# Two token halves pipelined in an eight-core decoder trunk: mixer or attention of one half interleaved with out-projection and FFN of the other

## The reference, cut to what matters

```python
# layer 1: Mamba-2 mixer, then ConvFFN; layer 2: attention, then ConvFFN
x = x + mamba2_mixer(rms_norm(x, a_norm), ...)   # in-proj to z,x,B,C,dt; causal conv of width 4; SiLU;
                                                 # chunked scan carrying a state over the tokens, 8 groups;
                                                 # gate with SiLU(z), group norm, out-proj 2048 -> 1024
x = x + conv_ffn(x, ...)                         # gate, val = rms_norm(x) @ w_in (1024 -> 2*2816)
                                                 # SiLU(causal conv of width 3 (gate)) * val, @ w_down
kv = rms_norm(x, kv_norm) @ w_kv + b_kv          # shared K/V, K normed and rotated
x = x + attention(...)                           # window 128, learned sinks, 16 query heads; out-proj
x = x + conv_ffn(x, ...)
```

## Time and profile before

| | |
|---|---|
| median of 3 runs | 2165.28 us (2155.01 to 2270.05) |
| profiled execution | 2161.5 us, span of its slowest core 2160.0 us |
| PE busy | 1840.8 us (85%) |
| DVE busy | 1266.3 us (59%) |
| ACT busy | 922.3 us (43%) |
| POOL busy | 578.7 us (27%) |
| chain that ended last | PE 66%, DMA 10%, DVE 8%, issue 7%, ACT 4% |

### The profile page before, as it was taken

One profiled execution on the slowest core, in us unless ns is written; L12 is line 12 of the kernel. 1 busy time (PEld: TensorE's weight loads), 2 busy tenths in 40 slices (PEclk: granted clock), 3 DMA queues, 4 the chain that ended last, 5 costly groups with the idle time before them and its releaser, 6 DMA issues.

```text
span 2160.0 us, 29050 instructions; the slowest of 8 cores (2109.5 to 2160.0 us)
## 1 busy us (share of the span) xinstructions
PE 1840.8 (85%) x9656; PEld 882.1 (41%) x9656; DVE 1266.3 (59%) x1863; ACT 922.3 (43%) x1380; POOL 578.7 (27%) x783
## 2 busy tenths in 40 slices
PE   1777887878878898999999995768587699999999
PEld 0344544545545443444444442223132344444444
DVE  2797787888878534653475324666567465325532
ACT  2557676757768313331133104564457333103310
POOL 2134464545645611000220022333222100000000
PEclk9898999999999999999999998989899899999999
DMA  9532343242335999543654449394853954375444
GB/s 206 129 60 52 52 71 53 44 68 51 52 61 137 194 163 126 98 79 64 110 91 78 74 78 102 59 108 68 69 88 64 93 88 78 64 156 83 78 74 112
DMA packets 220081, 193.05 MB, mean 89 GB/s; under 512 B 181408, under 2 KB 182688, under 8 KB 219936
## 3 DMA queue, kind: packets, MB, share of 16 engines
q0 software_dynamic: 32400, 115.42, 34.0%
q1 hardware_dynamic: 187536, 75.78, 21.2%
HBM read 254.65 MB, written 9.96 MB: 123 GB/s over the span
## 4 chain that ended last, share of the span: by engine, by line
PE 66%; DMA 10%; DVE 8%; issue 7%; ACT 4%; SPq 3%; POOL 2%; DVEq 0%; ACTq 0%; POOLq 0%
PE ps L238 66%; DMA hkv<-xnB_208 4%; SPq L324 3%; DMA hF_187<-xnF_191 2%; DVE acc_123 L278 2%; DMA hF_187<-xnF_190 1%; DVE acc_124 L278 1%; DVE att L267 1%; DMA xk_135<-xc_115 1%; SPq L317 0%; DMA yT<-yn_166 0%; DMA hT<-xnA_106 0%; DVE qT L267 0%; DVE dtot_211 L267 0%; DMA xin_84<-x 0%
## 5 line engine op out<-in xcount | busy, mean ns | idle before, releaser
L278 DVE SCALAR_TENSOR_TENSOR facc_192<-ps,cst,facc_192 128x1023 f32<-128x1023 f32 x88 | 112.8, 1281 | 60.7 <-ACT facc_192 L263 60.0
L278 DVE SCALAR_TENSOR_TENSOR facc_193<-ps,cst,facc_193 128x1023 f32<-128x1023 f32 x88 | 112.8, 1281 | 57.2 <-ACT facc_193 L263 56.4
L278 DVE SCALAR_TENSOR_TENSOR acc_123<-ps,cst,acc_123 128x1023 f32<-128x1023 f32 (+2 forms) x96 | 122.5, 1276 | 7.4 <-ACT acc_123 L263 7.3
L278 DVE SCALAR_TENSOR_TENSOR acc_124<-ps,cst,acc_124 128x1023 f32<-128x1023 f32 (+2 forms) x96 | 122.5, 1276 | 3.0 <-ACT acc_124 L263 2.3
L263 ACT ACTIVATE facc_192<-ps,cst 128x1024 f32<-128x1024 f32 x44 | 52.9, 1202 | 151.1 <-PE ps L238 151.1
L238 PE MATMUL ps<-cm 128*128 128x512 bf16 x252 | 102.2, 406 | 0.0
L263 ACT ACTIVATE sg_195<-facc_193 128x1024 bf16<-128x1024 f32 x44 | 46.5, 1057 | 129.9 <-DVE facc_193 L278 129.9
L263 ACT ACT_TABLE_LOAD x74 | 94.9, 1283 | 16.0 <-DVE acc_123 L278 8.8
L263 ACT ACTIVATE sg_194<-facc_192 128x1024 bf16<-128x1024 f32 x44 | 46.5, 1057 | 117.4 <-DVE facc_192 L278 117.2
L238 PE MATMUL ps<-hT,wr_60 128*128 128x512 bf16 x192 | 50.2, 406 | 52.4 <-DMA hT<-xnA_102 46.1
L267 DVE TENSOR_TENSOR u<-sg_195,ps 128x1024 bf16<-128x1024 bf16 x44 | 53.7, 1221 | 57.5 <-PE ps L238 50.3
(11 more groups left out here) (618 smaller groups left out, 4477.5 us busy)
## 6 DMA issues: line engine op xcount, KB each, us to landing
wr_63<-wfin POOLq DMA_DIRECT2D x18, 512.0 KB, 5.1
wr_61<-wfin POOLq DMA_DIRECT2D x18, 512.0 KB, 5.2
wr_62<-wfin POOLq DMA_DIRECT2D x18, 512.0 KB, 5.2
wr_64<-wfin POOLq DMA_DIRECT2D x17, 512.0 KB, 5.1
wr_60<-wfin POOLq DMA_DIRECT2D x17, 512.0 KB, 5.2
wr_60<-wfdn POOLq DMA_DIRECT2D x8, 512.0 KB, 5.1
wr_61<-wfdn POOLq DMA_DIRECT2D x8, 512.0 KB, 5.1
wr_62<-wfdn POOLq DMA_DIRECT2D x8, 512.0 KB, 5.1
```

The lines of the kernel that those rows point to most:

```text
L278: return self.add("dve", lambda e: e.scalar_tensor_tensor(out, in0, scalar, in1, op0, op1), rd, [out], self._c_dve(out, [in0, in1], "stt", ...
```

## The change

What it does, part by part:

1. Order. The mixer's units run half by half over all groups (`units` is now h outer, g inner). After the mixer of half 0 the program has four more stages: mixer half 1 with out-projection and FFN of half 0; attention blocks 0, 1 with out-projection and FFN of half 1; attention blocks 2, 3 with FFN of layer 2 of half 0; FFN of layer 2 of half 1 alone. All stage functions are generators that yield the modelled PE time of what they recorded; `inter` always advances the one that is behind.
2. PSUM. In a shared stage the FFN side has banks 0 to 3 (one pair for gate, one for value), the mixer or attention banks 4 to 7: one pair for P, bank 6 for decay, states and B-C products, bank 7 for y; attention has two banks for everything but the output.
3. Weights. Two rings, "A" with three slots and "F" with four. The mixer's 24 tiles are loaded once for each half.
4. `norm` scales with a tensor_scalar, transposes with 32 matmul transposes, and multiplies by the gain when PSUM is evacuated (ACT or DVE). Half 1 of the first norm keeps the DMA transpose (`norm_x`).
5. The FFN goes in thirds (8, 7, 7 channel tiles): gate, then a partial down-projection added to x; x is updated three times instead of once. The last FFN half keeps one pass and two pairs each.
6. Buffers: `xcB`, `bcB` two instead of three, head-norm sets two instead of four, one buffer for the rotary tables; scan states and y of half 1 go through HBM (`scr_st`, `scr_y`); K is stored by pairs of heads without zero padding.
7. The first x tiles are loaded ahead of the constants; the scheduler's modelled DMA costs are changed.

```diff
@@ schedule
-                if op.dma is not None:
+                if op.dmat:
+                    s0 = max(t + 0.45, dma_free)
+                    dma_free = s0 + op.dmat
+                    free_at[e] = max(t + c, s0 + 0.8)
+                    op.fin = dma_free + 1.3
+                elif op.dma is not None:
...
@@ weights
-    def wload(name, c0, n, shape):
-        slot = wcount[0] % NSLOT
+    def wload(name, c0, n, shape, ring="F"):
+        sl = rings[ring]
+        slot = wcount[ring] % len(sl)
...
+    def inter(*gens):
+        st = [[g, float(tot), 0.0] for g, tot in gens]
+        while st:
+            s = min(st, key=lambda v: v[2] / v[1])
+            w = next(s[0], None)
+            if w is None:
+                st.remove(s)
+                continue
+            s[2] += w
+            yield w
@@ norm
-                    K.stt(xv[:], tiles[i], rs[:, r, i:i + 1], grow, OP.mult, OP.mult)
-                    K.dmat(dst(i), xv[:], f"{sem}{i}")
+            K.ts(xn[i][:], tiles[i], rv[i], None, OP.mult)
+        for k2 in range(4):
+            pb = ps[:, nextbank(), :].bitcast(BF16).rearrange("p (k n) -> p k n", k=2)
+            for k in range(2):
+                for i in range(4):
+                    K.tr(pb[:, k, i * 128:(i + 1) * 128], xn[i][:, (2 * k2 + k) * 128:(2 * k2 + k + 1) * 128], ident)
+            for k in range(2):
+                for gname, dst in gains:
+                    K.evac(dst(2 * k2 + k), pb[:, k, :], scale=C(gname, 2 * k2 + k))
@@ mixer
-    units = [(g, h) for g in range(8) for h in range(2)]
+    units = [(g, h) for h in range(2) for g in range(8)]
+    PB = [(0, 1), (2,)]
+    SEG = [4, 6]
+    CBK = [7, 6]
+    wide = [True, False]
...
+    def A_gen(i0, i1):
+        for i in range(i0, i1):
+            if i == 6:
+                held["F"].extend([K.all_ops[-1]] * 4)
+            gens = [(S_gen(i), 10.4)]
+            if i + 1 < len(units):
+                gens.insert(0, (P_gen(i + 1), 20.8))
+            yield from inter(*gens)
@@ FFN
+    def gate(l, h, j, hb, uout, tg, tv):
+        w = wload(f"wfin{l}", j * 2048, 2048, (8, 256))
...
+    THIRDS = [(0, 8), (8, 15), (15, 22)]
+    def ffn_gen(l, h):
+        yield from norm_gen(l, h, hF)
+        for a, e in THIRDS:
+            for j in range(a, e):
+                yield from gate(l, h, j, hF, uF[:, j - a, :], 0, 1)
...
@@ the end
+    PE_A, PE_O, PE_F, PE_T = 248.0, 55.0, 228.0, 125.0
+    SKEW = 0.93
+    normA(0)
+    setup_A()
+    run(P_gen(0))
+    dt_half(0)
+    normA(1)
+    dt_half(1)
...
+    run(A_gen(0, 8))
+    run(inter((A_gen(8, 16), PE_A * SKEW), (chain(outp_gen(0), ffn_gen(0, 0)), PE_O + PE_F)))
+    setup_att()
+    run(inter((chain(att_gen(0), att_gen(1)), PE_T * SKEW), (chain(outp_gen(1), ffn_gen(0, 1)), PE_O + PE_F)))
+    run(inter((chain(att_gen(2), att_gen(3)), PE_T * SKEW), (ffn_gen(1, 0), PE_F)))
+    run(ffn_last(1, 1))
```

More of the change, by code:

```diff
@@ new lines, in norm_x @@
+    def norm_x(tiles, xn, junk, grow, dst, sem):
+        rv = norm_stats(tiles, junk)
+        for i in range(4):
+            xv = xn[xnc[0] % len(xn)]
+            xnc[0] += 1
+            K.stt(xv[:], tiles[i], rv[i], grow, OP.mult, OP.mult)
+            K.dmat(dst(i), xv[:], f"{sem}{i}")
+    yT = [K.sb(f"yT{q}", [128, 16, 512], BF16, Y0 + 16384 * q) for q in range(2)]
+    cur[0] = X1
+    hT = [K.sb("hT0", [128, 8, 1024], BF16, X0), alloc("hT1", [128, 8, 1024], BF16)]
+    cf = alloc("cf", [128, 256], F32)
@@ new lines, in build @@
+    stmp = allocn("stmp", [128, 256], F32, 2)
+    prevB = allocn("prevB", [128, 256], BF16, 4)
+    t1o = cur[0]
+    t1B = allocn("t1", [128, 2, 256], F32, 2)
+    ygB = allocn("yg", [128, 2, 256], BF16, 2)
+    ynB = allocn("yn", [128, 2, 4, 128], BF16, 2)
+    gjunk = alloc("gjunk", [128, 256], BF16)
+    ystB = allocn("yst", [128, 2, 512], BF16, 2)
+    K.a_end = cur[0]
+    junkA = [K.sb(f"junkA{i}", [128, 1024], BF16, t1o + 2048 * i) for i in range(2)]
+    growA = K.sb("growA", [128, 1024], F32, FM)
@@ new lines, in S_exp, with S_pre @@
+            K.act(e_[:].rearrange("p h l -> p (h l)"), bank(sg), AF.Exp)
+    def S_pre(i):
+        g, h = units[i]
+        pF = prevF[i % 2]
+        if h == 0:
+            K.memset(pF[:], 0.0, eng="pool")
+        else:
+            K.dma("sp", pF[:], scr_st[g].ap(), f"stl{i % 2}")
+        for ch in range(2):
+            K.ts(DdB[i % 2][:, ch, 0, :], ident, C("Dc", 2 * g + ch), None, OP.mult)
+            K.ts(DdB[i % 2][:, ch, 1, :], ident, Dlo[:, 2 * g + ch:2 * g + ch + 1], None, OP.mult)
@@ L1121, in build @@
+            tails.append((i, q))
+        if h == 0:
+            K.dma("sp", scr_st[g].ap(), prevF[i % 2][:], f"sts{i % 2}")
+        if i == len(units) - 1 or (h == 0 and g == 7):
             while tails:
                 S_tail(*tails.pop(0))
-    def xload(i):
-        K.dma("sp", xt[i][:], x_d[i * 128:(i + 1) * 128, :], f"x{i}")
-    def out_mm(kcs, m_list, banks, wts, dh, lhs, first, last, order="kc"):
-        pass
-    def accumulate(tiles, banks, nkc, ksplit, lhs, wget, fin):
-        for kc in range(ksplit):
-            for m, b in zip(tiles, banks):
-                K.mm(bank(b), lhs(m, kc), wget(kc), start=(kc == 0), stop=(kc == nkc - 1))
-        for m, b in zip(tiles, banks):
-            for kc in range(ksplit, nkc):
-                K.mm(bank(b), lhs(m, kc), wget(kc), start=(kc == 0), stop=(kc == nkc - 1))
-            fin(m, b)
@@ new lines, in gate @@
+    def gate(l, h, j, hb, uout, tg, tv):
+        w = wload(f"wfin{l}", j * 2048, 2048, (8, 256))
+        for n2 in range(2):
+            for kc in range(8):
+                K.mm(bank(2 * tg + n2), w[:, kc, 0:128], hb[:, kc, n2 * 512:(n2 + 1) * 512], start=(kc == 0), stop=(kc == 7))
+        yield 3.45
+        pg = pair(tg)
+        acc = facc[j % 2][:]
+        K.act(acc, pg, AF.Identity, bias=C(f"fcb{l}", j), scale=C(f"fcw{l}_2", j))
+        for s in (1, 2):
+            K.stt(acc[:, s:1024], pg[:, 0:1024 - s], C(f"fcw{l}_{2 - s}", j), acc[:, s:1024], OP.mult, OP.add)
+            if h == 1:
+                K.stt(acc[:, 0:s], halo_f[:, j, 2 - s:2], C(f"fcw{l}_{2 - s}", j), acc[:, 0:s], OP.mult, OP.add)
+        if h == 0:
+            K.copy(halo_f[:, j, :], pg[:, 1022:1024])
+        K.act(sgF[j % 2][:], acc, AF.Silu)
+        for n2 in range(2):
+            for kc in range(8):
+                K.mm(bank(2 * tv + n2), w[:, kc, 128:256], hb[:, kc, n2 * 512:(n2 + 1) * 512], start=(kc == 0), stop=(kc == 7))
+        K.tt(uout, sgF[j % 2][:], pair(tv), OP.mult)
+        yield 3.45
@@ new lines, in build @@
+    cur[0] = ATT
+    kT = alloc("kT", [128, 2, 1024], BF16)
+    vA = alloc("vA", [128, 8, 4, 128], BF16)
+    hkv = alloc("hkv", [128, 8, 512], BF16)
+    att = K.sb("att", [128, 8, 512], BF16, cur[0] - 8192)
+    hq = alloc("hq", [128, 8, 512], BF16)
+    qT = alloc("qT", [128, 8, 512], BF16)
+    csb = alloc("cs", [128, 2, 512], F32)
+    Pb = allocn("P", [128, 512], BF16, 4)
+    hn = []
+    for i in range(2):
+        a = alloc(f"qraw{i}", [128, 512], F32)
+        b = alloc(f"qrs{i}", [128, 512], F32)
+        c = alloc(f"qn{i}", [128, 512], BF16)
+        hn.append((a, b, b, c, c))
```

780 lines of the change are left out of this document (385 added, 395 removed).

## The result

The changed kernel is faster: the ratio of its time to that of the kernel before is 0.946, with an interval of 0.9408 to 0.9512. Its profiled execution took 2047.76 us, against the 2161.5 on which the forecast was made. (In three of its six executions the cores of one die or both had a lower mean granted clock, 0.89 to 0.95, in one execution of a later run even 0.80, and those three took 2105.85 to 2137.85 us; every comparison here leaves such executions out and goes by the others, here 2038.53 to 2047.76.) The forecast was 2025 us, 1945 to 2180.

What follows compares the result with a forecast made beforehand. PE has holes in mixer (streaming 74%) and attention but is busy in the FFN, so halves overlap. Stages 400 + 550 + 440 + 388 + 246 = 2024, with 1.5 outside the span 2025 us; range 1945 to 2180.

Steps and rivals of the forecast that it cites:

- the forecast's terms: Three shared stages with their two sides one after the other: 588, 472 and 417 us.
- No overlap 2167: Whole kernel if no shared stage overlaps: 420 + 588 + 472 + 417 + 270 = 2167 us.
- the rival of no overlap: Shared stages: scheduler orders by readiness and may run sides in turn, so no change; chance 0.16, shared with evacuation as bound.
- the line: Whole-kernel limits of the verdict: faster is below 2122 us, slower above 2208, same within 2%.
- the exposed norm: Norms between stages: chain stands 30.82, 34.45 and 38.60 us on DMA transposes, part of attention's unfilled time.
- The share of overlap realised: Three shared stages: a bit under half the possible gain, then the middle, giving 550, 440 and 388 us.
- the floors of 499, 409 and 354: Three shared stages in us if one half always has work ready, so PE streaming alone sets the time.
- Stage 5: Last FFN half alone: 231 us plus about 15 for its partly exposed first norm, 246 us.
- The evacuation rival: Shared stages: PSUM evacuations become the bound, 2175 us, no change; chance 0.16, shared with no overlap at all.
- The POOL rival: Shared stages: weight loads block POOL's queue for 602 us; if half reaches the path, 2326 us; chance 0.10.
- The clock rival: Last four stages: dense matmuls bring the granted clock to 0.89, 2210 us, or 2370 by the skill's 13/16; chance 0.04.
- stage 1: First half's mixer alone: start 86 us plus eight units at 39.4, 315, ending at 400 us, with 20 either way.

Runs made afterwards that it cites:

- the run on whole banks: Changed kernel with each shared stage's second side fenced behind the first, mixer and gates on their old PSUM banks; ratio 1.0744 to the kernel before.
- three small changes: Changed kernel with projection ahead of scan in units 0 to 6, first FFN loads spread, unit 8 projected on wide pairs; ratio 0.9322 to the kernel before.
- with the banks split: Changed kernel with each shared stage's second side fenced behind the first, the change's split of PSUM kept; ratio 1.1985 to the kernel before, 2590 us.
- The run with projection first: Changed kernel with each next unit's whole projection ahead of the scan in the mixer's first half; ratio 0.9461 to the kernel before, 2044.15 to 2050.29 us.

## Why the prediction was right, point by point

**The direction and the mechanism** were right: PE's holes in one half are filled from the other. In turn the same layout is 7% slower than before, with attention on its two banks.

**In turn, the forecast's terms** were 588, 472 and 417. Measured in the run on whole banks they are 595, 560 and 488. The mixer was sized well; attention was not: I took 89 us a block from the kernel before, at its clock of 0.89, but alone in this layout a block takes 124 to 128 at 0.74 to 0.77. (The stretch that gave 89 leaves out attention's two ends; from its first projection to the first gate matmul of layer 1 it is 382.38 us, 96 a block.) "No overlap 2167" should have been 2324 on whole banks and 2590 on the split ones that the change has, the slower side. It cost the forecast nothing, as most of the overlap was realised, but the rival of no overlap would have come out on the other side of the line. What I read as the exposed norm, the pieces of 30.82, 34.45 and 38.60 us, held 52 us of PE's waits and not 104.

**The share of overlap realised**, the step that I trusted least: above the floors of 499, 409 and 354 the stages ended 42, 9 and 46 us long, where I had allowed 51, 31 and 34. (At least 40 of stage 3's down-projection matmuls, some 9 us, run behind the cut at 1418, so the last two are better taken together, 55 for 65.) That it came out so well is luck in part. The allowance was about half of the way from the floor to the price in turn, and in the two attention stages that price was 88 and 71 us too low; half of the measured way would have been 75 and 67. More than half was realised, which made up for it. Stage 5 came out at 228.7 for 246: the transposes of its norm, 15 us in the forecast, ran for the most part before 1818, behind the last matmuls of stage 4. PE hardly waits in the shared stages. The longest sums of PE's waits from 460 to 1818 us:

```profile
PE ps L239 <- DVE acc_95 L279: 6.0, 4, 4.1
PE ps L244 <- DVE xnF_182 L274: 5.1, 2, 2.8
```

**The evacuation rival** falls with the same lines: `acc` is at the head, as named, but with 6.0 us in four waits, and PE is busy 95% of stage 2 where the rival had 80%.

**The POOL rival**: POOL was blocked nearly as long as feared and it didn't matter. Its waits for PE with a ring load at the head, from 459 to 1818 us:

```profile
POOL wf_56 L318 <- PE ps L239: 150.4, 24, 24.8
POOL wf_58 L318 <- PE ps L239: 150.1, 26, 23.4
POOL wf_57 L318 <- PE ps L239: 106.6, 22, 11.6
POOL wf_59 L318 <- PE ps L239: 95.9, 18, 17.3
```

That is 503.0 us in 90 waits, 5.6 each, for the 602 and 5.1 of the forecast. Little of it reached the path that counts: POOL has 1% of the chain, and PE, whose waits above are short, had the other half's matmuls ready.

**The clock rival**: 0.98 to 1.00 in stages 2 to 5 of the profiled execution. The 0.89 of the old attention stretch didn't show in it. Nor did the 13/16 that the Trainium skill states (TensorE: Matmul & The Clock Gate, Part 1) for dense matmuls on three cores of a die: no core's mean was under 0.956.

**The term that was mis-sized is stage 1**: "eight units at 39.4", with finer interleaving and two buffers "at nothing, with 20 either way". The start was right in size: the first transposes on TensorE ran at 11.28 us and the first projection at 28.83, for 46.12 before and some 26 in the forecast, and the z activation that ends unit 0 came at 71.1 instead of 94.5, 23 us earlier where I took 20. Then seven units took 48.1 us each (71.1 to 408.1), for 41.6 in the kernel before (94.5 to 385.6). The runs put 5.4 us a unit on the weave, some 17 us once on the burst of loads, and 35 on unit 8's narrow pair, which overlap in part; none of the three was in my sum, and the finer interleaving, which I thought might help, was what hurt most. I had named a cost of table loads only for the shared stages, and there PE hardly waited; it was in the mixer alone, with ACT the busiest it is anywhere, that it showed.

## What to carry to other kernels

An overlap has two prices. By the old kernel's stages it was 99 us here; by running the same layout in turn it was 310, since narrow banks and a lower clock are costs of the layout that only the overlap covers. What is gained on the old kernel is neither: 114 us by the profiled executions, of 136 forecast. A piece of the chain that stands on a DMA is not as much idle time of TensorE: 104 us of such pieces held 52 us of PE's waits, and the norms moved off the DMA queue gained 16. And look at the stage that has no partner: it got finer interleaving and the partner's first loads, and the projection of unit 8, which ends it, fell on the narrow pair, with no one to hide behind; three small changes there brought the ratio from 0.946 to 0.932.

## What the hardware showed that I had not expected

How far the clock falls in one stage and not in another. In one and the same kernel, in turn, the granted clock was 0.74 in attention, 0.94 in the mixer and 0.99 to 1.00 in the FFN, and 0.919 over the slowest core's whole span; with the banks split 0.89; overlapped 0.956. Attention's scores of 512 columns then took 554 ns in the mean, for 379. The Trainium skill (TensorE: Matmul & The Clock Gate, HAM oscillation — how this bites in real kernels) tells of a kernel whose waits between bursts send TensorE back to the lower clock each time. The run with projection first agrees: before three tiles of unit 8 PE waits 4.39, 3.10 and 5.50 us, and the matmuls of the tile then take 5.09, 6.55 and 5.57 us, for some 3.5 at the upper clock. So a stall can cost twice, once as time and once as slower matmuls behind it.

Attention in turn doesn't fit that account alone. Its lowest clock stands where PE doesn't wait at all (columns as in the earlier trace rows):

```profile
1260.30:1276.00 15.70, 15.70 (x32) 3.28 (x32) 6.29 (x10) 9.24 (x17) 0.00 (x0) 0.50 0.00 0
```

These are scores, masks and output one behind the other. The scores have K of 64 rows there, as the change stores K without zero padding; in the kernel before with norms on TensorE they have 128 rows, and took 382 ns in the mean in a stretch at 0.95. Overlapped with the FFN the scores of 64 rows took 386 ns. Whether the rows, the two banks or something else brings the clock down in turn no run separates; the overlap gave it back.
